# Retention values projected ahead of the retention gates, in a hybrid RWKV-7, retention and mixture-of-experts layer

## What is computed

```python
def retention_mix(z, gn_w):
    zf = z.astype(jnp.float32)
    q, k, v, g = jnp.split(zf, 4, axis=-1)
    ...
    q = rope(q)
    k = rope(k) * (HEAD_B ** -0.5)
    ...
    y = head_norm(y, GN_EPS_B).reshape(B_, L_, D_B) * gn_w
    return y * jax.nn.silu(g)
```

## Time and profile before

| what | us |
|---|---|
| median of 3 runs | 1355.05 |
| lowest and highest of the 3 | 1352.43, 1365.11 |
| the profiled execution | 1360.51 |
| its span, first to last instruction | 1358.5 |
| PE busy, share of the span | 1290.4, 95% |
| DVE busy | 1027.7, 76% |
| ACT busy | 715.3, 53% |

### The profile page before, as it was taken

The page is one execution under the profiler, slowest core; times in us unless marked ns, Lnnn a source line. Parts: engine busy times, 40 slices in busy tenths (PEclk is TensorE's granted clock), DMA queues, the critical chain, the costliest instruction groups (busy, mean ns, idle before and its releaser), DMA issues. The chain is left out here.

```text
span 1358.5 us, 23897 instructions
## 1 busy us (share of the span) xinstructions
PE 1290.4 (95%) x9822; PEld 1111.5 (82%) x9822; DVE 1027.7 (76%) x1145; ACT 715.3 (53%) x818; POOL 570.3 (42%) x210
## 2 busy tenths in 40 slices
PE   5999999999999989999989899999999999999994
PEld 5999999999899777888876678888888788888871
DVE  6356566589978256767777799998998997777775
ACT  6434324212342153333423777778777777777843
POOL 1011011000000032111111787778779879999974
PEclk8999999999999989999998999999999999999997
DMA  6136665772435595765647999999999999999978
GB/s 236 37 136 156 173 203 156 224 223 90 135 104 134 175 319 169 222 194 172 207 138 244 425 426 405 405 410 409 415 401 410 409 412 408 416 414 416 386 298 306
DMA packets 155508, 374.06 MB, mean 275 GB/s; under 512 B 53376, under 2 KB 108672, under 8 KB 143248
## 3 DMA queue, kind: packets, MB, share of 16 engines
q1 hardware_dynamic: 143328, 329.35, 66.4%
q0 software_dynamic: 6912, 25.17, 5.0%
q10 hardware_dynamic: 5184, 18.35, 3.3%
HBM read 299.67 MB, written 73.17 MB: 274 GB/s over the span
## 5 line engine op out<-in xcount | busy, mean ns | idle before, releaser
L1233 PE MATMUL ps<-u_hi,w_hi 128*128 128x352 f32 (+1 forms) x720 | 240.3, 334 | 5.0 <-DVE u_lo L888 4.9
L1233 PE MATMUL ps<-u_lo,w_hi 128*128 128x352 f32 (+1 forms) x720 | 235.9, 328 | 0.0
L1233 PE MATMUL ps<-u_hi,w_lo 128*128 128x352 f32 (+1 forms) x720 | 234.9, 326 | 0.0
L1233 PEld LDWEIGHTS ps<-u_hi,w_hi 128*128 128x128 f32 x720 | 139.6, 194 | 10.4 <-issue 5.9
L1233 PEld LDWEIGHTS ps<-u_lo,w_hi 128*128 128x128 f32 x720 | 139.3, 193 | 0.0
L1233 PEld LDWEIGHTS ps<-u_hi,w_lo 128*128 128x128 f32 x720 | 139.2, 193 | 0.0
L1687 POOL TENSOR_TENSOR mix_stat<-mix_stat,minus_half 128x4 f32<-128x4 f32 x8 | 10.7, 1334 | 289.7 <-DVE mix_stat L2063 289.7
L3315 PE MATMUL ps<-first_up_hi,x_hi 128*128 128x512 f32 x256 | 102.9, 402 | 3.4 <-PEq L197 2.1
L3315 PE MATMUL ps<-first_gate_hi,x_hi 128*128 128x512 f32 x248 | 97.3, 392 | 4.3 <-DVE x_lo L3092 3.8
L3315 PE MATMUL ps<-down_hi,hid_hi 128*128 128x512 f32 x248 | 99.3, 400 | 1.3 <-DVE hid_lo L3098 1.3
L3315 PE MATMUL ps<-first_up_hi,x_lo 128*128 128x512 f32 x256 | 100.2, 391 | 0.0
(11 more groups left out here) (475 smaller groups left out, 3440.3 us busy)
## 6 DMA issues: line engine op xcount, KB each, us to landing
first_down_raw<-in_moe_w_down SPq DMA_DIRECT2D x16, 2048.0 KB, 10.8
second_up_raw<-in_moe_w_up SPq DMA_DIRECT2D x16, 2048.0 KB, 9.5
down_raw<-in_moe_w_down SPq DMA_DIRECT2D x16, 2048.0 KB, 10.8
gate_raw<-in_moe_w_gate SPq DMA_DIRECT2D x15, 2048.0 KB, 10.2
up_raw<-in_moe_w_up SPq DMA_DIRECT2D x15, 2048.0 KB, 9.3
second_gate_raw<-in_moe_w_gate SPq DMA_DIRECT2D x15, 2048.0 KB, 10.3
y_slots<-y_out ACTq DMA_DIRECT2D x31, 512.0 KB, 11.3
w_raw<-in_w_in SPq DMA_DIRECT2D x30, 512.0 KB, 4.5
```

Of the source, the lines that this page charges most:

```text
L1233: mm = pe.matmul(z_of(n, r_), w[n % 3][:, k_, :], a[:, k_, c0:c1], start=(k_ == 0 and i == 0), stop=(k_ == KD - 1 and i == 2))
```

## The change

The order of `BLOCKS` becomes queries and keys, then the four value blocks (n = 22 to 25), then the four gate blocks (n = 26 to 29). Everything that is tied to a block number moves with it: the fills, ACT's copies, the transposes, the stores. The values now wait for `rope_products` 12 instead of 16, and the gates for 16. The second pair of keys is still emptied behind unit 2 of block 22 and unit 0 of block 23, which are value blocks now (`KEYS_EMPTIED`). The key stores get a semaphore for each pair. At the end of the projection the last block is a gate block, so a tanh, a scaled copy, `ret_gate(3)`, the transposes and the copy of the fills stand behind its last unit, and SP has no meta rows to store there. In the mixing the wait for the stored values goes, bh with kh is loaded ahead of rg, and rg behind a wait for its last odd store.

```diff
-BLOCKS += [("rg", i) for i in range(4)] + [("rv", i) for i in range(4)]
+BLOCKS += [("rv", i) for i in range(4)] + [("rg", i) for i in range(4)]
...
+    order += [("rv", i, f) for i in range(4) for f in range(2)]
     order += [("rg", i, f) for i in range(4) for f in range(2)]
-    order += [("rv", i, f) for i in range(4) for f in range(2)]
...
+KEYS_EMPTIED = 2
...
-                    if kind == "rg" and i > 0 or n == 26:
-                        j = i - 1 if kind == "rg" else 3
-                        sp.wait_ge(sem("tm_rg_ready"), 2 * (j + 1))
-                        store_tm("rg", j, tm_rg[j])
+                    if kind == "rv" and i > 0 or n == 26:
+                        j = i - 1 if kind == "rv" else 3
+                        sp.wait_ge(sem("tm_rv_ready"), 2 * (j + 1))
+                        store_tm("rv", j, tm_rv[j])
+                        store_meta(("rv", j))
...
-                sp.wait_ge(sem("tm_rv_ready"), 8)
-                store_tm("rv", 3, tm_rv[3])
-                store_meta(("rv", 3))
+                sp.wait_ge(sem("tm_rg_ready"), 8)
+                store_tm("rg", 3, tm_rg[3])
                 sp.wait_ge(sem("solved"), 1)
                 sp.dma_start(inv_dram.rearrange("h t (c s) k -> (h t c) s k", s=C), tri[:]).then_inc(sem("inv_stored"), 16)
...
+                def rows_turned(i):
+                    for f in range(2):
+                        turned(("rv", i), tm_rv[i], (f"tm_kd_stored{i // 2}", 16), f)
+                    meta_turned(("rv", i))
...
+                    elif kind == "rv":
+                        for r_ in range(3):
+                            if r_ == 0:
+                                if i < 2:
+                                    act.wait_ge(sem("rope_stored0"), 16 * 8)
+                                    act.wait_ge(sem("rope_products"), 12)
...
+                            plain(n, r_, rv[i % 2])
+                            if i == 0 and r_ == KEYS_EMPTIED:
+                                keys_turned(1, 0)
+                            if i == 1 and r_ == 0:
+                                keys_turned(1, 1)
+                            if r_ == 0 and i > 0:
+                                rows_turned(i - 1)
...
-                            if i == 0 and r_ == 2:
-                                keys_turned(1, 0)
-                            if i == 1 and r_ == 0:
-                                keys_turned(1, 1)
+                            if r_ == 0 and i == 0:
+                                rows_turned(3)
...
-                    dve.wait_ge(sem("zr_done"), UNIT_NO[22 + i, 2] + 1 - N_SH)
+                    dve.wait_ge(sem("zr_done"), UNIT_NO[26 + i, 2] + 1 - N_SH)
...
+                ret_gate(3)
...
-                        if kind == "rv" and i > 0 and r_ == 0:
+                        if (kind == "rv" and i > 0 or n == 26) and r_ == 0:
+                            j = i - 1 if kind == "rv" else 3
                             pe.wait_ge(sem("zr_done"), UNIT_NO[n - 1, 2] + 1 - N_SH)
-                            turn_block(("rv", i - 1), rv[(i - 1) % 2])
-                pe.wait_ge(sem("zr_done"), UNIT_NO[NB - 1, 2] + 1 - N_SH)
-                turn_block(("rv", 3), rv[1])
+                            turn_block(("rv", j), rv[j % 2])
+                pe.wait_ge(sem("rg_ready"), 4)
+                turn_block(("rg", 3), rg[1], meta=False)
                 keep_busy(pe, ps, cst, 3, 3)
...
-                sp.wait_ge(sem("tm_rv_stored"), 64)
                 load_tm(1, "v", "v")
                 load_tm(1, "a", "a")
                 load_tm(1, "kd", "kd")
                 load_tm(1, "rv", "rv")
                 sp.wait_ge(sem("inv_stored"), 16)
                 load_inv(1)
+                load_tm(1, "bh", "kh")
+                sp.wait_ge(sem("tm_rg_stored1"), 32)
                 load_tm(1, "rg", "rg")
-                load_tm(1, "bh", "kh")
```

More of the change, by code:

```diff
@@ L557, in _ @@
                     sp.wait_ge(sem(f"tm_{name}_stored"), tm_stores(name))
-                for i in range(2):
-                    sp.wait_ge(sem(f"tm_rg_stored{i}"), 32)
+                sp.wait_ge(sem("tm_rv_stored"), 64)
+                sp.wait_ge(sem("tm_rg_stored0"), 32)
                 for p in range(2):
                     sp.wait_ge(sem(f"rope_stored{p}"), 16 * 8)
-                sp.wait_ge(sem("tm_kd_stored"), 32)
+                    sp.wait_ge(sem(f"tm_kd_stored{p}"), 16)
                 sp.wait_ge(sem("zero_stored"), 16 * EXTRA)
@@ L796, in _ @@
                                 keys_turned(0, 1)
-                    elif kind == "rg":
+                    elif kind == "rv":
[4 more added lines that the diff above has]
+                                    act.wait_ge(sem("rope_products"), 12)
+                                    act.wait_ge(sem("filled"), FILL["kd", 0, 1, 1] + 1)
+                                    act.wait_ge(sem("meta_turned"), META_NO["kd", 0, 1] + 1)
+                                else:
+                                    act.wait_ge(sem("filled"), FILL["rv", i - 2, 1] + 1)
+                                    act.wait_ge(sem("meta_turned"), META_NO["rv", i - 2] + 1)
+                            plain(n, r_, rv[i % 2])
[5 more added lines that the diff above has]
+                                rows_turned(i - 1)
+                            if r_ == 1:
+                                split(n + 2)
+                    else:
                         for r_ in range(3):
@@ L817, in _ @@
                                         turned(("rg", i - 1), tm_rg[i - 1], RG_FREE[i - 1], f)
[L818 to L830, removed]
-                                for f in range(2):
-                                    turned(("rv", i - 1), tm_rv[i - 1], ("tm_kd_stored", 32), f)
-                                meta_turned(("rv", i - 1))
-                            if r_ == 1:
-                                if n + 2 < NB:
-                                    split(n + 2)
-                                if i == 0:
-                                    for f in range(2):
-                                        turned(("rg", 3), tm_rg[3], RG_FREE[3], f)
                 for f in range(2):
-                    turned(("rv", 3), tm_rv[3], ("tm_kd_stored", 32), f)
-                meta_turned(("rv", 3))
+                    turned(("rg", 3), tm_rg[3], RG_FREE[3], f)
             @block.gpsimd
@@ L1198, in _ @@
                             rope((n - 16) // 2)
-                        if kind == "rg" and i > 0 or n == 26:
-                            ret_gate(n - 23)
+                        if kind == "rg" and i > 0:
+                            ret_gate(i - 1)
                         if n >= 16:
```

21 lines of the change are left out of this document (10 added, 11 removed).

## The result

The kernel after takes 1363.66 us, median of 20 runs (1361.56 to 1368.74); the kernel before, measured 20 times beside it, 1358.27 (1352.43 to 1365.11). The ratio is 1.0041, 95% interval 1.0029 to 1.0053: 5.4 us slower, between 3.9 and 7.2. I had forecast 1356.3 in a range of 1350 to 1363, so both my level and my difference (+1.3) were too low. Of the level, 3.2 us are the 1355.05 of three runs, which twenty runs put at 1358.27; the other 4.1 are the change's.

What follows compares the result with a forecast made beforehand. PE was taken to bound the kernel almost alone, with the mixing's start set by SP's queue. The terms -2.02 + 1.88 + 1.4 gave +1.3 us, moving the median from 1355.05 to 1356.3, range 1350 to 1363.

Steps and rivals of the forecast that it cites:

- Step (a): End of block 22: PE's stall shortens by 0.44 us, 1.58 more if the clock holds; gain 2.02 us.
- Step (b): Turn behind unit 0 of block 23, now values: PE waits for the keys' second half; cost 1.88 us.
- Step (c): Projection's end: last turn and store 1.70 us later, inverses' issue 1.08 later, mixing's start taken as 1.4 later.
- Step (d): DVE's moved gate products, the inverses' solving, weight rounding, moved stores and new load order: no cost.
- Clock: Rival: clock lost at the two stalls in blocks 22 and 23 or the turn at the end; +4 us, chance 0.20.
- The first tiles at the lower clock: Rival: the later start makes the mixing's first tiles run at 1.2 GHz; up to 25 us, 1380, chance 0.03.
- Small gain: Rival: value block 0's turn hides and the mixing's start absorbs part of the delay; -1.3 us, 1353.7, chance 0.08.

Runs made afterwards that it cites:

- a_second: Kernel after with both halves of the last keys emptied behind unit 2 of block 22, where only the first was; ratio to before 1.0026.
- a_nofill: Kernel after without the three filler matmuls at the end of the projection; ratio to before 1.0035.
- a_loads: Kernel after with the load order undone: tile 1's gate rows loaded ahead of bh and kh again; ratio to before 1.0021.
- a_ki: Kernel after with the last keys emptied one unit earlier and the inverses' store first, new load order kept; 1352.69 us, ratio to before 0.9942.
- b_loads: Kernel before with only the new load order: tile 1's bh and kh loaded ahead of its gate rows; ratio to before 1.0012.
- b_keys: Kernel before with both halves of the last keys emptied one unit earlier, behind units 1 and 2 of block 22; 1355.6 us, ratio 0.9995.
- b_late: Kernel before with two filler matmuls in front of the turn of the last value block, delaying the projection's end; ratio to before 1.0021.
- a_keys: Kernel after with both halves of the last keys emptied one unit earlier, behind units 1 and 2 of block 22; 1360.30 us, ratio to before 1.0022.
- a_inv: Kernel after with the inverses' store issued ahead of the last gate block's store; ratio to before 1.0014.
- b_ki_newloads: Kernel before with the last keys emptied one unit earlier, the inverses' store first and the new load order; ratio to before 0.9968.
- a_kil: Kernel after with the last keys emptied one unit earlier, the inverses' store first and the old load order; ratio to before 0.9976.
- b_inv: Kernel before with the inverses' store put in front of the last values' store and their meta rows; ratio to before 0.9996.
- b_ki: Kernel before with the last keys emptied one unit earlier and the inverses' store first, old load order; 1353.68 us, ratio to before 0.9965.

## Why the prediction was wrong

**Step (a), end of block 22: right in the stall, half right in the clock.** From the last matmul to where the second unit would follow, it took 373.39 - 366.62 = 6.77 us (373.39 is 373.23 and the 0.16 of the next issue), forecast 6.76. But the 1.58 us for the clock I took from one execution. Over four profiles before loses it in three, so the gain in the mean is nearer 0.44 + 3/4 x 1.58 = 1.6 us than 2.02.

**Step (b), the turn of value block 0: right.** 376.17 - 373.23 - 0.16 = 2.78 us, forecast 2.67; a_second, which takes that stall away, gave back 1.88 us, forecast 1.88.

The last unit of the projection came 103.52 - 103.39 = 0.13 us later (forecast 0.14 earlier), and about 0.5 later than the mean of the four profiles with the old projection (103.39, 101.91, 103.41, 103.47).

**Step (c), the tail: right up to the meta products, and it ended too early.** From ACT's first look at the last unit, the last store came 1.7 us later (462.10 - 458.09 = 4.01 against 459.00 - 456.68 = 2.32), forecast 1.70; the inverses' issue 1.07 later, forecast 1.08; the meta products 1.47 later, forecast 1.4. The inverses landed at 462.51 + 9.2 = 471.7, which is 1.8 us later against the look: the 1.70 of the landing that follows the bytes ahead in the queue, and not the 1.08 of the landing that follows the issue. This is what the Trainium skill says of the order in a ring ("DMA: Bandwidth & Descriptors", Queues, rings and completion order), and here the trace agrees with it: 0.3 us more than I took. What I had not seen was that the fillers could run at half clock and hold the barrier by 1.6 us. In this execution they did, the meta load issued 2.2 us later instead of 1.1, and it cost nothing, as a_nofill shows, since the meta rows land behind the inverses. Of the seven profiles with these fillers behind the 2.25 us of idle, they were slow in three (after, a_loads, a_ki) and at full clock, 2.74 us, in four.

**The step that failed** is the sentence that the tiles and experts behind the start "are the same instructions and shift with it". They do not only shift: the clock behind the start changes as well. In all three profiles with the old seam and the full queue (before, b_loads, b_keys) it is 7.96 us from the meta products to `y_ret`; in the six with the later end it is 9.32 to 11.79, and b_late, which has only the delay, is at 9.31. From the last unit to `y_ret` the three take 21.0 us in the mean, and the four of the changed kernel's seam (after, a_loads, a_second, a_keys) 25.0. The 4.0 us are 1.7 us of the term (c) and 2.3 us of clock: PE is busy through all of the last stretch, at a clock of 1.00 in the three and of 0.57 to 0.82 in the four. My sum had this term at nothing, because I priced a loss there only as the rival of the first tiles. With the 0.5 of the projection the account is 4.5 us, against 5.4 measured (3.9 to 7.2). These are means over a few kernels with one profile each. Of the level, which is 7.4 us above the forecast, 3.2 us are no step of the sum but its base, the median of three runs.

**Step (d), at no cost: not contradicted**, as far as it was tried. The order of loads costs nothing that the mean of four pairs can tell. The cover of the inverses was there: in a_inv their store goes out at 453.61, right behind the one of 453.19. DVE's gates and the stores of blocks 23 to 26 were not tried by themselves.

**The rivals.** "Clock", at +4, was the nearest in size and named the wrong place: neither of the two stalls lost the clock, and the turn at the end took 1.09 us as before (1.58 in a_loads). It was lost at the fillers, where it is free, and behind the meta products, where it is not. "The first tiles at the lower clock" had the right place, and I had priced it as all or nothing over 40 us instead of a few us in which the clock is down; over the 40 us of rows 12 the clock in after is 0.97, where I had asked for 0.7. "Small gain" fell: both stalls are there. The list of signs said I would be wrong about the rest if the length from the meta load to the end changed by more than 2 us. It changed by 1.9 in the other direction (894.7 to 892.8), since from `y_ret` to the end the execution of after was 2.6 us shorter: the same 3810 matmuls of the mixing took PE 236.4 us at 0.98 instead of 241.0 at 0.96. The sign was too coarse, because later scatter of the clock lay on top of it.

What stays open: what decides whether the clock falls behind the meta products. A later start had it each time, but so had the two b_ kernels whose start came 2.4 us earlier (10.54, 10.51), and b_ki_newloads (11.18), while a_inv and a_kil, in between, kept it. So that a later start brings the loss is seen in these profiles and has no mechanism here. Idle time in front does not sort them: b_inv's meta products had no wait and a_keys's had 2.28 us. About 1 us of the 5.4 has no place; and by the medians the later end alone, b_late, gives 2.6 of the 5.4, with an interval from -0.1 to 6.0.

## What to carry to other kernels

A step that moves the start of a stage is priced beyond that start: read the granted clock of the first 10 us behind it, and ask of a term for the clock on both sides. Where one queue carries the last store and a large transfer that the next stage waits for, try the large one first as soon as its data is there. By itself this gained 0.27% in the kernel after (a_inv, with intervals that overlap) and nothing that can be told in the kernel before (b_inv); with the keys one unit earlier it took the kernel before from 0.9995 to 0.9965 and the kernel after from 1.0022 to 0.9942, and with it the order of the blocks, which had cost 0.4%, no longer showed a cost that all pairs agree on. And before a difference of a few us is read from two profiles, see where each lies in the runs of its kernel; here the pair showed 1.6 us of 5.4.

## What the hardware showed that I had not expected

- The same stall of 1.8 us, in the same code, was followed by the lower clock in three executions and not in the fourth. The turn behind it took 1.61 us in before, 1.51 in b_late and 1.29 in b_loads. The Trainium skill has it that the number of slow matmuls varies from run to run of one kernel ("TensorE: Matmul & The Clock Gate", Part 1); the trace agrees.
- Two idle stretches one unit apart, 1.37 and 1.46 us, cost no clock in any of the five profiles that have both.
- Fillers in front of a barrier are no protection when they themselves run slow: 4.44 us for six pieces instead of 2.74, and PE was released 1.46 us behind them. Whether that costs anything was decided by the transfer that the next stage needs: nothing in after, 1.70 us in a_ki against a_kil.
- The 2 MB of inverses took 8.5 us to land behind the values' store, 9.2 when issued 0.4 us behind the last 512 KB, and 6.5 and 7.9 where they were issued ahead of it (b_ki, a_ki).
